# A convolution mixer computed by token halves, with three diagonal buffers, and the turns of an MLP dealt out as four, eight and four

## The reference, cut to what matters

```python
CONV_WIDTH = 31

def _conformer_conv_mixer(h, w_in, dw_w, dw_b, ln_g, ln_b, w_out):
    a, b = jnp.split(h @ w_in, 2, axis=-1)
    u = a * jax.nn.sigmoid(b)
    u = lax.conv_general_dilated(u, dw_w[:, None, :], window_strides=(1,),
                                 padding=[(CONV_WIDTH - 1, 0)], ...,
                                 feature_group_count=D_MODEL) + dw_b
    mu = jnp.mean(uf, axis=-1, keepdims=True)
    var = jnp.mean(jnp.square(uf - mu), axis=-1, keepdims=True)
    un = (uf - mu) * lax.rsqrt(var + NORM_EPS) * ln_g + ln_b
    return jax.nn.silu(un) @ w_out

for i in range(DEPTH):                       # mixers: nsa, stick-breaking, conv, moba
    x = x + mixer_i(_rms_norm(x, attn_norm[i]))
    hm = _rms_norm(x, mlp_norm[i])
    x = x + jnp.square(jax.nn.relu(hm @ mlp_w_up[i])) @ mlp_w_down[i]
```

## Time and profile before

| | |
|---|---|
| three runs | 3345.96, 3346.24, 3359.56 us; median 3346.24 |
| the profiled execution | 3356.01 us; span of the core 3354.3 us; mean granted clock 0.99 |
| busy | PE 3227.4 us (96%), DVE 1933.2 (58%), ACT 1627.4 (49%), POOL 199.0 (6%) |
| the convolution's taps to the next stage's first transpose | 2762.22 to 2857.81 us |

### The profile page before, as it was taken

The page is one execution under the profiler, slowest core; times in us unless marked ns, Lnnn a source line. Parts: engine busy times, 40 slices in busy tenths (PEclk is TensorE's granted clock), DMA queues, the critical chain, the costliest instruction groups (busy, mean ns, idle before and its releaser), DMA issues.

```text
span 3354.3 us, 52004 instructions
## 1 busy us (share of the span) xinstructions
PE 3227.4 (96%) x19601; PEld 2822.5 (84%) x19601; DVE 1933.2 (58%) x2856; ACT 1627.4 (49%) x2425; POOL 199.0 (6%) x258
## 2 busy tenths in 40 slices
PE   7999999998999999999999999899999999999999
PEld 7977988977998978897987897779788887887797
DVE  4656546565555654655556556565466566655663
ACT  4445445444444435544445445544354455545552
POOL 1001001000001000101000102000000000102100
PEclk9999999999999999999999999999999999999999
DMA  6653656642565643565554654435544550555364
GB/s 218 194 176 123 200 182 189 200 151 89 169 194 175 194 155 117 157 192 178 185 186 146 182 184 150 135 113 187 181 135 154 187 181 13 187 183 170 112 202 150
DMA packets 413278, 551.69 MB, mean 164 GB/s; under 512 B 33952, under 2 KB 263520, under 8 KB 413104
## 3 DMA queue, kind: packets, MB, share of 16 engines
q1 hardware_dynamic: 409248, 536.10, 49.8%
q0 software_dynamic: 2864, 10.38, 1.0%
q10 hardware_dynamic: 992, 2.84, 0.2%
HBM read 548.15 MB, written 1.05 MB: 164 GB/s over the span
## 4 chain that ended last, share of the span: by engine, by line
PE 86%; DVE 9%; ACT 3%; issue 1%; POOL 0%; DMA 0%; SPq 0%; DVEq 0%; ACTq 0%
PE G L799 15%; PE G L803 15%; PE G L800 15%; PE G L900 11%; PE G L901 11%; PE G L902 11%; DVE ring_lo_sb L1915 4%; PE T L775 2%; PE S L994 1%; PE O L1022 1%; DVE act_hi_sb L1929 1%; DVE act_lo_sb L1939 1%; PE G L1302 1%; ACT ring_hi_sb L1402 1%; DVE work_sb L2116 0%
## 5 line engine op out<-in xcount | busy, mean ns | idle before, releaser
L1915 DVE TENSOR_TENSOR ring_lo_sb<-ring_sb,ring_hi_sb 128x1024 fp32r<-128x1024 f32 (+1 forms) x998 | 1200.9, 1222 | 610.8 <-ACT ring_hi_sb L1402 592.4
L1402 ACT ACTIVATE ring_hi_sb<-ring_sb 128x1024 fp32r<-128x1024 f32 (+1 forms) x1028 | 1056.0, 1044 | 681.1 <-DMA ring_sb<-ffn_w_down 217.0
L900 PE MATMUL G<-act_hi_sb,ring_hi_sb 128*128 128x256 f32 x3136 | 877.1, 280 | 3.0 <-DVE ring_lo_sb L1915 3.0
L901 PE MATMUL G<-act_lo_sb,ring_hi_sb 128*128 128x256 f32 x3136 | 874.2, 279 | 0.0
L902 PE MATMUL G<-act_hi_sb,ring_lo_sb 128*128 128x256 f32 x3136 | 873.5, 279 | 0.0
L799 PE MATMUL G<-ring_hi_sb,hid_hi_sb 128*128 128x512 f32 x1456 | 582.5, 400 | 13.8 <-DVE hid_hi_sb L1948 6.5
L900 PEld LDWEIGHTS G<-act_hi_sb,ring_hi_sb 128*128 128x128 f32 x3136 | 589.5, 188 | 3.4 <-issue 3.2
L902 PEld LDWEIGHTS G<-act_hi_sb,ring_lo_sb 128*128 128x128 f32 x3136 | 589.1, 188 | 0.0
L901 PEld LDWEIGHTS G<-act_lo_sb,ring_hi_sb 128*128 128x128 f32 x3136 | 588.7, 188 | 0.0
L800 PE MATMUL G<-ring_lo_sb,hid_hi_sb 128*128 128x512 f32 x1456 | 578.5, 397 | 0.0
L803 PE MATMUL G<-ring_hi_sb,hid_lo_sb 128*128 128x512 f32 x1248 | 493.2, 395 | 0.0
(11 more groups left out here) (264 smaller groups left out, 2608.9 us busy)
## 6 DMA issues: line engine op xcount, KB each, us to landing
ring_sb<-ffn_w_gate_up SPq DMA_DIRECT2D x704, 256.0 KB, 3.9
ring_sb<-ffn_w_down SPq DMA_DIRECT2D x352, 256.0 KB, 3.7
ring_sb<-mlp_w_up SPq DMA_DIRECT2D x256, 256.0 KB, 3.6
ring_sb<-mlp_w_down SPq DMA_DIRECT2D x256, 256.0 KB, 3.7
ring_sb<-a_w_in SPq DMA_DIRECT2D x48, 256.0 KB, 4.3
ring_sb<-sb_w_in SPq DMA_DIRECT2D x48, 256.0 KB, 3.9
ring_sb<-moba_w_in SPq DMA_DIRECT2D x48, 256.0 KB, 4.1
ring_sb<-w_mem_kv SPq DMA_DIRECT2D x32, 256.0 KB, 3.8
```

The costliest lines, as they stand in the source:

```text
L900: mm(dst, hi, act_hi[:, kt, :], start=(kt == 0 and f == 0), stop=False, skip_group_check=True)
L901: mm(dst, hi, act_lo[:, kt, :], start=False, stop=False, skip_group_check=True)
L1402: fn(ring_hi[:, s_, :, 0:w], ring[:, s_, :, 0:w], ACT.Copy).then_inc(hi_ready, 1)
L1915: v.tensor_tensor(ring_lo[:, s_, :, 0:w], ring[:, s_, :, 0:w], ring_hi[:, s_, :, 0:w], ALU.subtract).then_inc(lo_ready, 1)
```

## The change

**What it does.** (1) The first ten taps of tile 4 go from TensorE to VectorE, which adds them on top of what ScalarE took out of PSUM; the diagonals of a tile are split into two near halves and a third buffer of 16 is added, so that a group waits for the group three before it. (2) Tile 7 is convolved by token halves on TensorE, and everything behind it (mean, squares, power, spread, Silu, splits, output product) is done for half 0 and then for half 1, each step of a half placed among other work of TensorE: steps of half 0 among the taps of half 1, steps of half 1 among the output products of half 0. The output product takes all eight units for half 0 and then for half 1. (3) VectorE no longer splits units 0 and 1 of the next stage ahead of its first addition to `x`; it splits units 0 to 2 behind it and ahead of the turned activations, unit 3 between their high and low parts. (4) In the MLP the 16 transposes are issued as four ahead of chunk 2, eight in its middle and four behind it, and the copies of ScalarE and VectorE are moved with them. The paired form of the same code, used by the other feed-forward stages, keeps its order. Cut to its core:

```diff
+SHARED = 10
+        more_diags = sb("more_diags", [P, DIAGS, P], over="hid_hi")
-        conv_sums = [S[:, 0, :], O[:, 0, :], G[:, 0, 0, 0:SEQ], G[:, 1, 0, 0:SEQ]]
-        diag_groups = [(k, i, min(DIAGS, CONV_W - i)) for k in range(CONV_PE, KT) for i in range(0, CONV_W, DIAGS)]
+        conv_sums = [S[:, 0, :], O[:, 0, :], G[:, 0, 0, 0:SEQ]]
+        conv_halves = [G[:, 1, t, 0:P] for t in range(TT)]
+        def diag(at):
+            return more_diags if at % 3 == 2 else diags[:, at % 3]
+        for k in range(CONV_PE, KT):
+            first = SHARED if k == CONV_PE else 0
+            middle = first + -(-(CONV_W - first) // 2)
+            diag_groups += [(k, first, middle), (k, middle, CONV_W)]
+            if kind == "conv":                    # last_of
+                return OUT_K[kind]
...
 TensorE, up_down
+                    turn_hidden(0, paired, tb, 0, 0, g + 1, only=0)
+                    turned_half(0, 0, paired, n + 2 * CHUNK_UNITS, g + 1)
+                    turn_hidden(0, paired, tb, 0, 0, g + 1, only=1)
+                    turn_hidden(1, paired, tb + per, 0, 0, g + 2, only=0)
+                    turned_half(1, 0, paired, n + 2 * CHUNK_UNITS, g + 1)
+                    turn_hidden(1, paired, tb + per, 0, 0, g + 2, only=1)
...
 TensorE, conv
+                def half_taps(t, at, first, end):
+                    k, begin, _ = diag_groups[at]
+                    for tap in range(first, end):
+                        last = mm(conv_halves[t], diag(at)[:, tap - begin, :],
+                                  conv_in[:, k, t * P + tap:t * P + tap + P], start=(tap == 0), stop=(tap == CONV_W - 1))
+                half_taps(0, at_a, 0, cut_).then_inc(mix_full, 1)
+                pe.wait_ge(diag_ready, at_b + 1)
+                half_taps(0, at_b, cut_, CONV_W).then_inc(mix_full, 1)
+                mean(0)
+                half_taps(1, at_a, 0, cut_)
+                sums(0)
+                half_taps(1, at_b, cut_, cut_ + 8)
+                spread_out(0)
+                half_taps(1, at_b, cut_ + 8, CONV_W).then_inc(mix_full, 1)
+                mean(1)
+                for t in range(TT):
+                    for k in range(KT):
...
+                        elif k == 2:
+                            sums(1)
+                        elif k == 4:
+                            spread_out(1)
...
 VectorE, residual
-                        if post:
+                        if post or stages[s][0] == "conv":
                             ahead(c["unit"] + 3)
...
 VectorE, conv
-                taps(two, 0, CONV_W)
+                taps((*two, CONV_PE), 0, SHARED)
+                taps(two, SHARED, CONV_W)
+                centre(0)
+                ahead(c["unit"] + RING - 1)
+                deviation(0)
+                scaled(0, 0)
+                scaled(0, 1)
+                halves(0, 0)
...
```

More of the change, by code:

```diff
@@ L1304, in taps @@
                         last.then_inc(mix_full, 1)
[L1306 to L1311, removed]
-                    return last
+                def half_taps(t, at, first, end):
+                    k, begin, _ = diag_groups[at]
+                    for tap in range(first, end):
+                        last = mm(conv_halves[t], diag(at)[:, tap - begin, :],
+                                  conv_in[:, k, t * P + tap:t * P + tap + P], start=(tap == 0), stop=(tap == CONV_W - 1))
+                    return last
@@ new lines, in sums, with spread_out @@
+                def sums(t):
+                    bank = t_open(c["T"])
+                    for a_ in range(2):
+                        pe.wait_ge(squares_in, 2 * t + a_ + 1)
+                        for k in range(4):
+                            last = mm(bank[:, 0:1], hid_cols[:, a_, k, t * P:(t + 1) * P], ones[:, 0:1],
+                                      start=(a_ + k == 0), stop=(a_ + k == 4))
+                    last.then_inc(t_full, 1)
+                    c.up("T")
+                def spread_out(t):
+                    bank = t_open(c["T"])
+                    pe.wait_ge(spread, t + 1)
+                    mm(bank[:, 0:P], ones, nrm[:, t, 0:P], start=True, stop=True).then_inc(t_full, 1)
+                    c.up("T")
@@ L1314, in conv @@
                 for k in range(CONV_PE, KT - 1):
                     taps(k)
[L1316 to L1330, removed]
@@ L1487, in up @@
                     mem_turns(1)
-                turned_copies(1)
+                turned_copies(1, range(per - 1, per))
                 split_chunk(4)
@@ new lines, in _ @@
+                    summed(CONV_PE)
+                    ahead(c["unit"] + RING)
+                    diagonal(3)
+                    diagonal(4)
+                    summed(CONV_PE + 1)
+                    diagonal(5)
+                    diagonal(6)
+                    summed(CONV_PE + 2)
+                    diagonal(7)
+                    summed(KT - 1, 0)
+                    squares(0)
+                    link(fn(conv_out[:, 0, 0:1], ident[:, 0:1], ACT.Silu))
+                    factor(0)
@@ L1888, in _ @@
+                    silus(0, 0)
+                    summed(KT - 1, 1)
+                    silus(0, 1)
+                    squares(1)
+                    silus(0, 2)
+                    silus(0, 3)
+                    factor(1)
+                    for p_ in range(KT // 2):
+                        silus(1, p_)
+                    c["T"] = tb + 8
                     c.up("unit", KT)
@@ new lines, in taken, with centre @@
+                def taken(m):
+                    dve.sem_inc(t_taken[m % 2], 1)
+                def centre(t):
+                    m, ts = tb + 2 + 3 * t, slice(t * P, (t + 1) * P)
+                    dve.wait_ge(t_full, m + 1)
+                    for a_ in range(2):
+                        tiles = conv_acc[:, 4 * a_:4 * a_ + 4, ts]
+                        v.scalar_tensor_tensor(tiles, over(t, 4), -1.0 / D, tiles, ALU.mult, ALU.add).then_inc(centred, 1)
+                    dve.wait_ge(centred, 2 * t + 2)
+                    taken(m)
```

234 lines of the change are left out of this document (126 added, 108 removed).

## The result

| | before | after |
|---|---|---|
| median of 16 runs each | 3359.43 us (3345.96 to 3365.79) | 3344.55 us (3330.30 to 3352.41) |
| profiled execution | 3356.01 us | 3332.71 us |
| ratio after / before | | 0.9955, 95% interval 0.9943 to 0.9966 |

By this series the change saves 14.9 us (11 to 19), where I had forecast 12.6. The measured median, 3344.55, lies outside the forecast's own range of 3328 to 3340 and only just inside the wide one of 3325 to 3346.

A forecast was written before the change was run, and what follows sets the result against it. TensorE, busy 3227.4 of 3354.3 us, was taken to bound the kernel. The stage's -11.5 and the next opening's -1.1 gave -12.6 us, from 3346.24 to 3333.6 us, 0.38% faster; own range 3328 to 3340, wide range 3325 to 3346.

The forecast's parts named there:

- The stage: Convolution mixer up to the next opening: taps, diagonal waits, norm and output product together -11.5 us.
- narrow tile 7: Tile 7's taps on TensorE: 124 instructions of 0.111 us for 62 of 0.216, +0.4 us, bounds -0.4 and +9.5.
- waits for diagonals: TensorE waits for ScalarE in tiles 5 and 7, since shorter tile 4 cuts its lead: +3.9 us, bounds 0 and +6.
- waits of the norm: Behind the convolution's taps: halving and interleaving turn 7.8 us of waits into 0.3, so -7.5, bounds -7.8 and -3.
- output product's clock: Start of the mixer's output product: first twelve products at full clock take 2.8 us for 5.20, -2.4.
- Loads not hidden: Rival on tile 7's narrow taps: weight loads make each take 0.188 us, +9.5, giving 3343.1 us; chance 6%.
- The clock: Rival on tile 7 to the output product: waits and sparse products bring 1.2 GHz, +36.5 us, 3370.1; chance 5%.
- Turns wait: Rival in the four MLPs: last turns come too soon and weights late, +12 us, 3345.6, no change; chance 7%.
- More than forecast: Rival in the convolution stage: ScalarE keeps ahead, no wait for diagonals, -3.9 us more, 3329.7; chance 6%.
- The margins: VectorE's taps in the convolution: ten more end at 2806.0, TensorE asks at about 2809.8, hidden with 3.7 us to spare.
- The next opening: Next stage's start: one split fewer between high and low parts closes TensorE's wait, -1.1 us, bounds -1.2 and 0.
- The MLPs: Transposes in three groups instead of two win nothing: 0 us, bounds -0.4 and +2 for each of four MLPs.

The follow-up runs named there:

- experiment 6: The kernel after with no tap of tile 4 given to VectorE; first tap to transposes 87.81 us, +4.33.
- experiment 8: The kernel after with ScalarE's four splits moved behind the last diagonals, and tile 6's sum behind those; 3341.21 us, ratio to before 0.9939.
- experiment 5: The kernel after with all 62 instructions of tile 7's second half ahead of the first half's mean; first tap to transposes 90.70 us, +7.2.
- experiment 7: The kernel after without the early splits of the next stage's units; first tap to transposes 86.62 us, +3.1, and +0.8 to the MLP's first turn.
- experiments 1, 11 and 12: The kernel before with the MLP's turns alone: 0.9993; nine shared taps on top of experiment 8: 0.9952; the same with turns as eight and eight: 0.9966.
- after_again: The kernel after once more, unchanged; 3337.06 us, ratio to before 0.9942.
- experiment 12: The kernel of experiment 8 with nine shared taps instead of ten and the MLP's turns as eight and eight; 3344.70 us, ratio to before 0.9966.
- experiment 2: The kernel after with the MLP's turns put back to eight and eight; 3348.63 us, ratio to before 0.9976.

## Why the prediction was right, and where it was not

**The stage.** The forecast was -11.5 us, the profile shows -12.1. By its terms:

| term | forecast | measured | from |
|---|---|---|---|
| taps of tile 4 | -4.3 | -4.2 | 9.18 for 13.39; experiment 6 gives 4.3 too |
| narrow tile 7 | +0.4 | +0.7 | 124 instructions in 14.06 |
| means | +0.1 | 0.0 | 3.49 for 3.46 |
| waits for diagonals | +3.9 | +3.0 | 1.63 and 1.37 for 2.0, 1.6 and hand-overs |
| waits of the norm | -7.5 | -7.8 | none left |
| sums with a column of ones | -1.0 | -1.2 | 2 x 1.70 for 4.59 |
| spread | -0.7 | -0.7 | 0.30 and 0.14 for 1.19 |
| output product's clock | -2.4 | -2.2 | 22.6 for 24.8 |

The measured ones add up to -12.4; 0.3 stay in hand-overs between groups. The bound that decided most, whether loads of 0.188 hide beside 128 columns, came out on the side of the earlier trace rows: 3.58 / 32 = 0.112 us for each. So the rule of the Trainium skill that I weighed (in "TensorE: Matmul & The Clock Gate", Part 3, "The mechanism": loads overlap only with matmuls on other row groups) does not hold for this form. The same section also lets a load be pulled ahead where it goes to the background weight buffer; I had left that out, and the trace, with loads of 0.19 us hidden 0.112 apart, fits it. With loads not hidden the 124 would have cost 9.5 more.

**The diagonals.** Their waits came near the forecast size, 3.0 for 3.9, but the cause that I gave for the first, a shorter tile 4 and less lead for ScalarE, is wrong: with tile 4 at its full length it was 1.82 us, longer and not gone (experiment 6). It comes of the order of ScalarE's list, four splits between tile 4's sum and tile 5's last diagonals, and it went when they were moved (experiment 8). That the size was near is in part luck.

**The rivals.** Loads not hidden: no. The clock: not in the kernel after, but experiment 5 shows that it was real: take the dense taps from between the steps, and 0.50 is back. Nor was the wait of 2.32 us in the earlier trace rows, at 1.00, a safe sign against it: in experiment 7 one of 2.97 was followed by 0.50. Turns wait: no wait at any. More than forecast: ScalarE didn't keep ahead.

**The margins.** I gave VectorE's taps 3.7 us of cover. TensorE came to them at 2801.3 and VectorE had ended at 2799.5: 1.8. VectorE was 1.8 later against the first tap than before (its last taps' start 17.1 behind it, not 15.4), since TensorE had come sooner to the stage's taps than VectorE did. It cost nothing here, because TensorE waited 3.0 for diagonals; experiment 8 took that cover away and found the end of the margin at once.

**The next opening.** Forecast -1.1; measured -0.7 (transposes to the MLP's first turn 25.94 for 26.64). The wait for the low parts went, as said, and 0.17 of a late unit came, within the bounds; that the moved split is the cause is argued from VectorE's order and not shown by a run (experiment 7). What I had missed is the other side of those lines: without them the reordered output product costs 4.0 (experiment 7). The step on that said that the first half's rows would be ready some 5 us ahead; that holds only because the splits were moved.

**The MLPs.** This step failed: I took 0 with bounds of -0.4 and +2 for each, from the transposes' own 0.9 us. Eight transposes cost no wait, but the loop behind them never took its short pitch; behind four it did in 17 of 32. That is 1.1 us for each MLP on average, 4.6 together, by the count; the time shows it nowhere by itself (experiments 1, 11 and 12). It isn't a wait, an idle time or a clock, and none of the views that I had read for waits shows it; the count of products in equal stretches does.

**The sum.** -12.1 - 0.7 - 4.6 = -17.4 us is what the parts give; the runs say -14.9 (11 to 19), and for `after_again` -19. The forecast of -12.6 lacks the last of these parts; that it lies as near to -14.9 as it does is helped by the runs' giving less than the parts. Experiment 12, the stage's part without the turns and with 2.5 us more, has -11 (6 to 17) where its profile gives -15; experiment 2 has -8 (3 to 13) where its profile gives -12.6. Both hold it, the second only at its edge. Whether something outside the stage takes a little back is open; I found no wait that the kernels with the convolution part have and the others don't. The two first profiled executions differ by 23.3 since, besides the parts, three MLP loops and one gated loop more, 9.9 us, were short in the second.

## What to carry to other kernels

A chain of small dependent steps is best hidden by cutting it in two and laying the other half's dense work between the steps: it closes the waits and keeps the clock. Cutting alone left 4.68 of 7.83 us of waiting and the low clock; dense work between uncut steps wasn't tried. An order in which one engine's side work (splits of coming weights) stands ahead of what the bounding engine wants next should be looked at again after every reordering, both here and at the next stage. And where a time scatters by some tenths of a per cent from run to run, count the instructions of one form in equal stretches before explaining a difference: a busy engine isn't one that runs at one rate.

## What the hardware showed

- The same 256-column products, with their weight loads, at the same granted clock of 1.00 and with no gap, come every 117.8 or every 113.3 ns (mean duration 279 and 276 ns), one of the two for a whole loop. It changes from execution to execution of one program; with 3.45 us for each of the gated loops it makes up a good part of the scatter of 20 us between runs of the kernel before. Of the loops behind one group of transposes that follows products of the same form, only those behind four or six were ever short, never those behind five, seven, eight, nine or ten; nor were the products behind four transposes at a later stage's opening. But it was short in 2 of 14 first gated loops, behind eight transposes, a wait and four, and in the stick-breaking mixer in 4 of 14 stretches behind a wait of 0.5 us with no transposes. What sets it, and whether it can be had every time, is open.
- Where 3.14 us of waiting stood behind 1.54 and thin products, the clock fell to 0.50 (experiment 5); with single waits of 1.63 and 1.37 between dense taps it stayed at 1.00. Behind a wait of 2.97 us, eight transposes and one of 0.35 it was at 0.50 too, although dense products at 1.00 stood ahead (experiment 7), while a wait of 2.32 in the last mixer left it at 1.00.
